# A hybrid decoder step: filler work carried over the ends of the stages, weight casts given to ScalarE, and the causal mask added on GpSimd instead of TensorE

## What is computed

```
h = rmsnorm(x) @ w_in         # fox q,k,v,f,z | hgrn q,f,i,z | mem q,z | three gates of 1024
fox:  softmax(q k^T / 8 + c_q - c_k, causal) v      # 8 heads x 64, c = cumsum(log f)
hgrn: S = f S + (1-f) v ; o = q S                   # 4 heads, 128x128 state
mem:  softmax(q mk^T / sqrt(128)) mv                # 4 heads x 128, 256 memory rows
mixed = sig(ga) * ((o_fox * silu(z)) @ w_pa) + sig(gb) * (rmsnorm(o_hg) ... @ w_pb) + sig(gm) * (... @ w_pm)
y = rmsnorm(x + mixed @ w_o)
```

## Time and profile before

| | |
|---|---|
| median of 3 runs | 3064.44 us (3054.81 to 3074.55) |
| the profiled execution | 3058.63 us; its span 3056.9 us |
| TensorE busy | 2802.7 us, 92% |
| weight loads (PEld) | 2295.1 us, 75% |
| VectorE, ScalarE, GpSimd busy | 1583.8, 1036.8, 811.6 us (52%, 34%, 27%) |
| mean granted TensorE clock | 0.961 |
| DMA | 528.44 MB, 173 GB/s on average |

### The profile page before, as it was taken

One profiled execution on the slowest core, in us unless ns is written; L12 is line 12 of the kernel. 1 busy time (PEld: TensorE's weight loads), 2 busy tenths in 40 slices (PEclk: granted clock), 3 DMA queues, 4 the chain that ended last, 5 costly groups with the idle time before them and its releaser, 6 DMA issues. The chain is left out here.

```text
span 3056.9 us, 38630 instructions
## 1 busy us (share of the span) xinstructions
PE 2802.7 (92%) x13880; PEld 2295.1 (75%) x13880; DVE 1583.8 (52%) x3023; ACT 1036.8 (34%) x1972; POOL 811.6 (27%) x846
## 2 busy tenths in 40 slices
PE   7899998999995989999779999999999977999998
PEld 5678776667774878787658888888887865888887
DVE  5415676343443446556426665666664545444544
ACT  2211111332321334344225555555554234232322
POOL 6058885344244252533350020020020000000000
PEclk9999998999997999999889999999999998999999
DMA  5587778566544657666575455554443545433331
GB/s 168 222 257 230 233 249 277 186 176 185 174 136 143 200 194 244 205 219 200 176 223 155 138 147 160 156 160 142 139 139 114 198 170 173 131 107 117 116 109 49
DMA packets 292430, 528.44 MB, mean 173 GB/s; under 512 B 110398, under 2 KB 135551, under 8 KB 270991
## 3 DMA queue, kind: packets, MB, share of 16 engines
q1 hardware_dynamic: 239967, 408.13, 42.5%
q0 software_dynamic: 16656, 53.36, 6.0%
q10 hardware_dynamic: 35616, 64.47, 5.5%
HBM read 413.19 MB, written 112.68 MB: 172 GB/s over the span
## 5 line engine op out<-in xcount | busy, mean ns | idle before, releaser
L2452 PE MATMUL fill_out<-fill_w_hi,fill_x 128*128 128x512 f32 x2112 | 739.1, 414 | 94.3 <-POOL fill_w_lo L2545 45.0
L2452 PEld LDWEIGHTS fill_out<-fill_w_hi,fill_x 128*128 128x128 f32 x2112 | 393.7, 193 | 174.4 <-POOL fill_w_lo L2545 58.9
L2452 PE MATMUL fill_out<-fill_w_lo,fill_x 128*128 128x512 f32 x1056 | 438.1, 415 | 0.0
L461 DVE TENSOR_TENSOR fox_pt_lo<-fox_turned,fox_pt_hi 128x512 fp32r<-128x512 f32 (+1 forms) x320 | 194.8, 609 | 157.1 <-ACT fox_pt_hi L408 155.3
L2086 ACT ACTIVATE in_stage<-in_out 128x512 f32<-128x512 f32 (+1 forms) x119 | 70.9, 597 | 593.7 <-PE in_out L99 546.3
L408 ACT ACTIVATE fox_pt_hi<-fox_turned 128x512 fp32r<-128x512 f32 (+1 forms) x320 | 170.1, 531 | 300.8 <-PE fox_turned L358 299.1
L447 DVE CUSTOM_DVE_ANT_0 fox_probs<-fox_scores,fox_bias 128x512 f32<-128x512 f32 (+2 forms) x320 | 187.5, 608 | 93.1 <-PE fox_scores L347 50.6
L2543 POOL CAST fill_w_hi<-fill_raw 128x512 fp32r<-128x512 f32 x80 | 51.5, 644 | 678.5 <-PE fill_out L2463 643.5
L2452 PEld LDWEIGHTS fill_out<-fill_w_lo,fill_x 128*128 128x128 f32 x1056 | 204.6, 194 | 30.5
L97 PE MATMUL in_out<-x_first,ring_hi 128*128 128x512 f32 x512 | 201.0, 393 | 7.4 <-POOL ring_lo L2007 7.4
L99 PE MATMUL in_out<-x_first,ring_hi 128*128 128x512 f32 x512 | 200.5, 392 | 0.0
(11 more groups left out here) (356 smaller groups left out, 5932.8 us busy)
## 6 DMA issues: line engine op xcount, KB each, us to landing
fill_x<-x_tiles SPq DMA_DIRECT2D x132, 1024.0 KB, 5.4
dc_slot<-in_cache_fox_k_dram SPq DMA_DIRECT2D x128, 256.0 KB, 3.9
dc_slot<-in_cache_fox_v_dram SPq DMA_DIRECT2D x128, 256.0 KB, 3.1
in_raw<-in_w_in_dram POOLq DMA_DIRECT2D x104, 256.0 KB, 4.0
plain<-fill_stage ACTq DMA_DIRECT2D x96, 256.0 KB, 5.4
mf_gate<-plain SPq DMA_DIRECT2D x96, 256.0 KB
turned<-in_stage ACTq DMA_DIRECT2D x64, 256.0 KB, 3.9
fill_raw<-in_w_in_dram POOLq DMA_DIRECT2D x64, 256.0 KB, 3.0
```

Of the source, the lines that this page charges most:

```text
L461: dve.tensor_tensor(pt_lo[:, b, skip:BANK], bank_of(st)[:, skip:BANK], pt_hi[:, b, skip:BANK].bitcast(F32), ALU.subtract).then_inc(turned_ ...
L2452: ins = pe.matmul(self.out[n % self.OUTS][:], x, w, start=(k == 0 and term == 0), stop=(ends and term == 2))
```

## The change

It has six parts.

1. **Mask.** The matmul of line 350 goes. GpSimd adds the mask to the 512 entries of the keys' bias of a quad (four row tiles) with one instruction, into `masked_bias` (two buffers, `mask_bias`). VectorE makes the diagonal 128 columns of a tile with an instruction of its own that reads `masked_bias`; 96 of the 128 last blocks so become two instructions. VectorE waits for `bias_masked`, GpSimd for the scores of the quad two before.
2. **Weights carried over.** The filler's weights lie in `keep_hi` and `keep_lo`, half of the projection's ring, held over the stages; its first group is split in the last pass of the projection stage. The first slots of the recurrence hold matmuls now, the masks are built in its third step, and SyncE loads the first x tile before anything else.
3. **Casts by ScalarE.** In the projection stage and in the recurrence ScalarE makes the high part (`high`, `high_by_scalar`) and GpSimd only the low one (`low`). The projection stage has three raw buffers instead of two, and splits the slices of a pass of the first half two to a unit. Three steps of the paged attention's middle (`m`) come one or two units later.
4. **Filler counts.** The recurrence has 1340 matmuls spread and 96 after its last chunk, while VectorE and SyncE finish its rows; the attention 144 in its first nine slots, 1472 spread, 10 and 12 around its last `back`; the memory stage 16 at its very start and 206 in 17 slots. The two memory groups of 48 come one gate group later.
5. **Attention's start.** TensorE waits for the constants only at the first score, and head 1's queries and values are loaded there too.
6. **Merge.** GpSimd loads, casts and subtracts the 16 slices of `w_o` in two buffers (in `gains`, whose own load comes last); SyncE, ScalarE and VectorE have no work for them.

```diff
-    steps += [("out", *quads[-1]), ("back", *quads[-1])]
+    TAIL = FILLS + 2 * FH * J_HEAD
+    steps += [("out", *quads[-1]), ("fill", TAIL), ("back", *quads[-1]), ("fill", TAIL + 1)]
...
+                def mask_bias(n):
+                    head, q = quads[n]
+                    pool.wait_ge(bias_loaded, 16 * (head + 1))
+                    if n >= 2:
+                        before, p = quads[n - 2]
+                        pool.wait_ge(scores_used, before * S_HEAD + S_AT[4 * p + 3] + CHUNKS[4 * p + 3])
+                    pool.tensor_tensor(masked_bias[n % 2][:],
+                                       bias[:, q * BANK:(q + 1) * BANK].rearrange("p (i n) -> p i n", n=P),
+                                       mask[:].unsqueeze(1).to_broadcast([P, 4, P]), ALU.add).then_inc(bias_masked, 1)
+
+                for n in range(2):
+                    mask_bias(n)
+                for st in steps:
+                    if st[0] == "fill":
+                        fill.gpsimd(pool, st[1])
+                    if st[0] == "score" and st[2] % 4 == 3 and st[3] == CHUNKS[st[2]] - 1:
+                        n = quad_at[st[1], st[2] // 4] + 2
+                        if n < len(quads) and n % QUADS >= 2:
+                            mask_bias(n)
...
-                        if c == CHUNKS[i] - 1:
-                            last = pe.matmul(out[:, width - P:width], ident_r[:], mask_r[:], start=False, stop=True)
...
+                        if c == CHUNKS[i] - 1:
+                            dve.wait_ge(bias_masked, quad_at[h, i // 4] + 1)
...
+                        last = c == CHUNKS[i] - 1
+                        parts = [(0, width - P * last, bias[:, c * BANK:c * BANK + width - P * last])]
+                        if last:
+                            parts = [part for part in parts if part[1] > 0] + [(width - P, width, masked_bias[quad_at[h, i // 4] % 2][:, i % 4, :])]
+                        for n, (first, end, by) in enumerate(parts):
+                            ins = dve.tensor_tensor_reduce(probs_of(i, c * BANK + first, c * BANK + end),
+                                                           scores[s % S_BANKS][:, first:end], by, 1.0, NEG, ALU.add, ALU.max,
+                                                           most[:, slot, c + n:c + n + 1])
+                        ins.then_inc(scores_used, 1)
...
-        fill.begin([0] * 2 * SPLITS + fill.spread(matmuls, 2 * (len(chunks) + AHEAD - SPLITS)))
+        fill.begin(fill.spread(matmuls, 2 * (len(chunks) + AHEAD)) + fill.spread(last_matmuls, TAIL), True)
...
+                fill.sync_start(sp)
                 load_unit(0)
+                fill.sync_next(sp)
...
+                    if n == 2 - AHEAD:
+                        build_masks()
...
-        fill.begin(fill.spread(matmuls, NT))
+        fill.begin([first_matmuls] + fill.spread(matmuls - first_matmuls, NT + 1))
...
-    PASSES, STAGES, OUTS, RAWS = 2, 4, 4, 2
+    PASSES, STAGES, OUTS, RAWS = 2, 4, 4, 3
...
+        def split_at(m):
+            n, k = divmod(m, KT)
+            if ring_before[m] is not None and ring_before[m] // KT == n - 1:
+                return n * U - 1
+            return (n - 1) * U + (k // 2 if n < G else k)
...
+                def low(m):
+                    hi, lo = w_ring.at(ring_at[m])
+                    pool.wait_ge(cast, m - KT + 1)
                     pool.tensor_tensor(lo, raw[m % RAWS][:], hi.bitcast(F32), ALU.subtract).then_inc(split, 1)
-                    if m + RAWS < N * KT:
-                        pool.wait_ge(split, 2 * (m - KT) + 2)
+                    if m + RAWS < SLICES:
...
+                def high(m):
+                    act.wait_ge(raw_loaded[m % RAWS], 16 * ((m - KT) // RAWS + 1))
+                    ring_free(act, m)
+                    act.activation(w_ring.at(ring_at[m])[0], raw[m % RAWS][:], ACT.Copy).then_inc(cast, 1)
...
+    def high_by_scalar(self, act, n):
+        self.wait_slice(act, n)
+        act.activation(self.w_hi[:, n % KT, :], self.raw[n % self.RAWS][:], ACT.Copy).then_inc(self.cast, 1)
...
+                for i, (kk, n) in enumerate(last_slices):
+                    at = slice(n * BANK, (n + 1) * BANK)
+                    pool.wait_ge(late_loaded[i % 2], 16 * (i // 2 + 1))
+                    pool.tensor_copy(w_hi[:, kk, at], late_raw[i % 2]).then_inc(late_split, 1)
+                    pool.wait_ge(late_split, 2 * i + 1)
+                    pool.tensor_tensor(w_lo[:, kk, at], late_raw[i % 2], w_hi[:, kk, at].bitcast(F32), ALU.subtract
+                                       ).then_inc(late_split, 1)
+                    if i + 2 < len(last_slices):
+                        pool.wait_ge(late_split, 2 * i + 2)
+                        load(i + 2)
+                pool.wait_ge(late_split, 2 * len(last_slices))
+                pool.dma_start(gains[:], gain.partition_broadcast(P)).then_inc(gains_loaded, 16)
 
...
-MATMULS = {"recur": 1600, "first": 100, "fox": 1396}
+MATMULS = {"recur": 1340, "recur_last": 96, "fox_first": 144, "fox": 1472, "fox_last": [10, 12], "memory_first": 16}
...
-        groups = [plain_group(name) for name in LATE] + gate_groups[:2] + memory_groups + gate_groups[2:]
...
+            groups = [plain_group(name) for name in LATE] + gate_groups[:3] + memory_groups + gate_groups[3:]
```

369 lines of the change are left out of this document (214 added, 155 removed).

## The result

Over 20 runs each the changed kernel takes 3050.45 us (3039.69 to 3059.87) and the kernel before 3072.36 us (3054.81 to 3085.77): ratio 0.9931, interval 0.992 to 0.9942.

The account below looks back on a forecast made before the run. TensorE was taken as busy nearly throughout, with idle time mainly at stage changes. Seven terms saved 128 us from 3058.6; with half of 5.8 given back, 2933 us, range 2890 to 2985 (all low ends: 3016).

Parts of the forecast that it names:

- Projection stage: Projection: casts on ScalarE end most weight-ring waits, and later middle steps end a paged-attention wait; 28 us saved (12 to 35).
- I take 17 of the 20.0 us: Projection: faster slices on GpSimd would remove 17 of the 20.0 us that TensorE waits on the weight ring.
- Start of the recurrence: From projection to first chunk: no slice awaited and 97 filler matmuls ahead, 19 us lost instead of 44; 25 saved (15 to 30).
- The rival of the fixed part: Stage changes keep their fixed idle time, halving the gains at the recurrence's and attention's starts; 2961 us, chance 0.18.
- Group changes: Filler group changes in the recurrence: faster slices cut TensorE's waits for low halves; 12 us saved (none to 25).
- Start of the attention: From recurrence to attention: filler after the last chunk covers the block change, idle 11.5 us for 43.2; 34 saved (22 to 42).
- idle there 4.5 instead of 24: Between TensorE's last recurrence chunk and the attention block: 96 filler matmuls would leave 4.5 us idle instead of 24.
- Mask: Attention: dropping 128 mask matmuls saves TensorE 8 us; 15 lost if VectorE's extra 23 us all lie on the path.
- The rival of the handshake: Attention: GpSimd's mask additions wait for the next head's bias and VectorE waits for them; 2979 us, chance 0.09.
- Memory stage: Memory stage: filler matmuls placed in the waits for the store and keys; 7 us saved (3 to 9).
- Merge: Merge: TensorE no longer waits for 16 slices of w_o; 14 us saved (6 to 17) after 3 for contention.
- Slower by ScalarE's casts: Projection and recurrence: ScalarE's casts, waiting for loads, delay its evictions and so TensorE; 3096 us, chance 0.03.

Follow-up runs that it names:

- best_casts_on_pool: Changed kernel with the edits of setup_first, x_early, kept_early, one_slice and three_raws, plus the projection's casts back on GpSimd: 3003.6 us, against 3007.2 without that last edit.
- middle_back: Changed kernel with the edits of setup_first, x_early, kept_early, one_slice and three_raws, plus the paged attention's middle steps at their old units: 2997.5 us.
- best_all: The kernel of middle_back with the projection's casts back on GpSimd too: 3003.4 us, ratio 0.9772.
- setup_first: Changed kernel, but in the projection's first unit GpSimd does the sample path's setup ahead of the two weight slices: 3040.4 us, ratio 0.9912.
- one_slice: Changed kernel with one weight slice to a unit, not two, in the projection's early passes: 3043.4 us, ratio 0.9912.
- kept_early: Changed kernel with the projection's last eight slices, for the filler's first group, made two to a unit and so three to four units earlier: 3042.3 us.
- x_early: Changed kernel with x tiles nearer the front of SyncE's queue at the starts of the recurrence and the attention: 3039.0 us, ratio 0.9907.
- casts_on_pool: Changed kernel with the casts of the filler's slices in the recurrence back on GpSimd: 3060.9 us, ratio 0.9961.
- three_raws: The kernel of mask_on_pe with a third raw buffer for the filler's weight slices: 3032.9 us, against mask_on_pe's 3046.8.
- mask_on_pe: Changed kernel with the mask matmuls back on TensorE and one VectorE instruction per score tile, no mask added by GpSimd: 3046.8 us, ratio 0.992.

## Why the prediction was wrong, step by step

- **Projection stage, -28, measured +23.** This is the step that failed. "I take 17 of the 20.0 us" rested on GpSimd's 2.82 us a slice as the only limit. The waits on the ring did go (20.0 to 0.6 us). What it left out is the other chain into TensorE, the sample path: its waits grew by 27 us, evictions took 7, and the pauses made the same matmuls 8.5 us slower. With the later middle best_casts_on_pool shows the casts to be worth nothing, because the sample path collects what they free; with the middle as before (middle_back, best_all) they may be worth 14, so the term's size stays open, and the change had paired them with the middle that spends it. The new order cost 14 us in the first unit (setup_first) and up to 14 in the early passes (one_slice; together 19). Nowhere had I asked what stands behind the first subtraction on GpSimd, or what two slices to a unit do to the products there. The 7 us of the step "The 8.2 us wait of the paged attention's middle gets a unit of 7.1 us (800 / 112) more" were lost again by `dc_sums` behind `sr_part`.
- **Start of the recurrence, -25, measured -16.** "The block's first loads left 5 us after TensorE's last matmul, and this stays" was wrong by 4.7 us, GpSimd's DRAIN (kept_early), and the "1 to 3 us of waits" for x tiles were 8.9 (x_early). The rival of the fixed part is this in size, which had halved the gain of both starts; its path, a store behind the tail, is seen at the other one.
- **Group changes, -12, measured +4.** The low halves gave their 12 us (19.8 to 7.2). The term put nothing for evictions behind the casts, and these took 21. It had named two raw buffers as a bound and put it at 2.7 us a slice from an undisturbed landing of 3.0; in the recurrence ScalarE waits 17 times and 38.8 us for landings, the longest 5.2. ScalarE's casts are worth 10 us (casts_on_pool), a third buffer 14 with the attention's part (three_raws).
- **Start of the attention, -34, measured -8, or -18 on the forecast's stretch.** That "the block may end 2 to 3 us later" came as 4.7, by the store behind the tiles. The "idle there 4.5 instead of 24" left out the queue: the tile stands behind ten loads, 11.5 us, of which x_early takes back 6. The waits at the memory group (12.9 us in four at 1816 to 1856) are the 48 matmuls moved to the middle, which I had counted as covered; three_raws has some 4 there.
- **Mask, -8, measured about -1.** The price on VectorE was 7.4 and not 23, TensorE's gain 10; but the saved time turned into waits for VectorE's scores and for the low half (mask_on_pe). The rival of the handshake didn't show: in the trace neither VectorE nor another engine waits for GpSimd's additions (line 236).
- **Memory stage, -7, measured -1.** The wait of 9.4 for mem_v is gone; the block change, queries and an x tile take 2.2, 1.9 and 3.7 us.
- **Merge, -14, measured -8.** Right mechanism; the contention was 7.7 us on VectorE and 5.1 in TensorE's waits for it, not 3, and within the forecast's bound of 11. The rest of the gap isn't traced.
- **Slower by ScalarE's casts.** Decided at 0.94 us a cast; it came only at two group changes, 18.6 us, and the same casts pay for it.

The range ended at 2985, short even of the 3016 that all my low ends give. And the low ends themselves, the mask's apart, assumed that a part could at worst gain little or nothing, none that a stage whose order was rewritten could lose. With +23 for -28 in one term the rest of my low ends (31) would have given about 3050; that this meets the measured time is partly luck, since the single terms miss their low ends on both sides.

## What to carry to other kernels

When the order in a queue changes, list what stands behind the first instruction that now waits, on that engine and on those that it feeds, before counting what the wait's end brings. A wait removed from one chain is worth only what the next chain into the same engine is early by; here a second chain (small work on VectorE, fed by loads) took all of it back in one setting and none in another. A store at a block's end, and GpSimd's DRAIN, belong on the list of what must end before the next block. And before work is moved between engines to speed up a pipeline, try one more buffer: two changed numbers gave as much as this whole change.
